# A mixture-of-experts layer: half the depth of the down product as three rounded products, the low part of its weights by GpSimd

## The chip, the cores and the metric

The kernel runs on one core of one Trainium2 chip. The metric is the device time of one execution in microseconds. Before the change it is 1408.04 us, the median of 3 runs (1407.59 to 1409.12). The profile is one further execution. PE is TensorE, DVE is VectorE, ACT is ScalarE, POOL is GpSimd and SP is the engine that issues most DMAs.

## The reference, cut to what matters

One encoder layer: a token mixer, and then a mixture of experts with top-8 routing over 64 experts and one shared expert. Only the routed experts are touched:

```
def expert_block(args):
    xb, e = args
    return (jax.nn.silu(xb @ we_gate[e]) * (xb @ we_up[e])) @ we_down[e]
```

There are 512 tokens of 1024 channels, so 4096 assignments; the hidden width of an expert is 256. `we_gate[e]` and `we_up[e]` are 1024x256, `we_down[e]` is 256x1024, all float32. Each result is scaled by its gate and summed per token.

## The kernel before

The function `experts` works through blocks of up to 128 tokens that go to one expert. There are 64 blocks, one for each expert, and here four more for experts with over 128 tokens: 68. For a block the kernel finds its token numbers with a one-hot product, gathers the tokens' rows from HBM (POOL, `gather`), turns them (PE, `turn_x`), multiplies them with gate and up (PE, `gate_up`), applies silu and the product (ACT `sigmoid`, DVE `silu` and `hidden`), turns the hidden rows (PE, `turn_hidden`, one turned tile per half k of the 256 hidden channels), multiplies with the down weights (PE, `down`), copies the result out of PSUM in two halves (ACT and DVE, `y_half`) and scatters the rows to HBM (POOL, `scatter`).

Gate and up products are made in parts: ACT rounds a float32 operand to the type fp32r (`high`), DVE subtracts that from the operand and rounds the rest (`low`), and PE adds high·high, low·high and high·low. Each of these is a rounded product. The down product is exact: both operands are float32.

Each engine has its own program, a list of stages with a lead: in step b the stage with lead 2 works on block b + 2. `steps` writes these lists out for the first blocks, runs the rest up to block 59 in a counted loop, and blocks 60 to 67 in a loop with conditions. There POOL also waits at the end of each step until the scatter of that step has landed (the argument `last` of `steps`, called by `scattered`). The order of a list is the order in which its engine works; nothing reorders it. Semaphores join the lists.

Weights stand in rings of four slots that SP fills: gate and up of block b once the products of block b - 4 are done, down likewise. Every gather and scatter has a one-element addition on POOL ahead of it, `carrier` (L2123), which carries the waits.

Of the kernel before, what the change touches and what calls it, by code (L numbers as in the profile page):

```python
# [20 lines left out]
F32R = mybir.dt.float32r  # L21
# [7 lines left out]
P = 128  # L29
# [40 lines left out]
class Memory:  # L70
# [1865 lines left out]
def plan_experts(nc, m, w, keep, moe):  # L1936
# [38 lines left out]
def experts(nc, w, keep, moe):  # L1975
# [4 lines left out]
    with ExitStack() as stack:  # L1980
# [9 lines left out]
        sig = m.sb("sig5", [P, 2, DE])  # L1990
        hid = m.sb("hid", [P, 2, DE])
        hT = m.sb("hT5", [P, 2, 2, P])
# [18 lines left out]
        s_h, s_hA = m.sem("p5_hidden_turned"), m.sem("p5_hiddenT")  # L2011
# [14 lines left out]
        def steps(engine, stages, last=None):  # L2026
# [89 lines left out]
        def _(pool):  # L2116
# [25 lines left out]
            steps(pool, [(4, gather), (0, scatter)], lambda b, u: scattered(pool, b, u))  # L2142

        @block.scalar
        def _(act):
# [10 lines left out]
            def sigmoid(b, u, first):  # L2156
                act.wait_ge(s_gu, b + 1)
                taken(act, s_hid, b, 2)
                act.activation(sig[:, u % 2, :], pgu[u % 2][:, 0:DE], ACT.Sigmoid).then_inc(s_sig, 1)
# [8 lines left out]
            def hiddenT(b, u, first):  # L2168
                act.wait_ge(s_h, b + 1)
                taken(act, s_y, b, 2)  # L2170
                act.activation(hT[:, u % 2, :, :], ph[:, 0:2 * P].rearrange("p (k s) -> p k s", k=2), ACT.Copy).then_inc(s_hA, 1)  # L2171
# [6 lines left out]
            steps(act, [(2, high(0)), (2, high(1)), (0, hiddenT), (2, high(2)), (2, high(3)), (1, sigmoid), (2, x_high), (0, y_half)])  # L2178

        @block.tensor  # L2180
        def _(pe):
# [28 lines left out]
            def turn_hidden(b, u, first):  # L2210
                pe.wait_ge(s_hid, b + 1)
                taken(pe, s_hA, b, 1)
                rows = hid[:, u % 2, :].rearrange("p (d k) -> p k d", k=2)
# [11 lines left out]
            def down(b, u, first):  # L2225
                pe.wait_ge(s_hA, b + 1)
# [3 lines left out]
                weights = moe.down[:, u % RING, :, :]  # L2230
# [279 lines left out]
```

## Time and profile before

| | |
|---|---|
| median of the runs | 1408.04 us |
| the profiled execution | 1406.37 us, span 1404.6 us |
| PE busy | 1297.7 us, 92% |
| DVE busy | 1010.8 us, 72% |
| ACT busy | 617.2 us, 44% |
| POOL busy | 256.0 us, 18% |
| blocks of the experts | about 650 to 1340 us of the span |
| exact down products, L2233 | 544 records, 8 for each block: 2 for each of 4 products |

A record of PE overlaps the next, so the time that a product takes from PE is the distance between two starts, not the length of a record. "idle before" stands in square brackets, with what ended the idle time. A row of the timeline can hold several instructions (x2); its length then reaches from the first start to the last end.

### The profile page before, as it was taken

What the parts mean: (1) busy time and instruction counts of PE and PEld (TensorE: products, weight loads), DVE (VectorE), ACT (ScalarE), POOL (GpSimd) and SP (SyncE); (2) the same over time, 40 slices, a digit from 0 to 9 for tenths busy, and PEclk for the clock granted to TensorE, in tenths of its full rate; (3) what the DMA queues carried; (4) which work ended last, traced back from release to release, by engine and by line L of the source; (5) the groups of instructions that cost most, each with busy time, mean ns of one, the idle gap of its engine ahead of it and who ended that gap; (6) DMA issues with size and microseconds to landing.
All of it is one profiled execution on the core that took longest, in us unless ns stands there. A gap on an engine that the chain in (4) does not pass through costs nothing. (4 is left out here: it accounts for less than half of the span.)

```text
span 1404.6 us, 18781 instructions
## 1 busy us (share of the span) xinstructions
PE 1297.7 (92%) x5779; PEld 914.4 (65%) x5779; DVE 1010.8 (72%) x1651; ACT 617.2 (44%) x944; POOL 256.0 (18%) x329
## 2 busy tenths in 40 slices
PE   4999999858998999969999999999999999999947
PEld 4878888546884444536767677676776767776613
DVE  5879999789343523646878888788887888878617
ACT  3523222542242013134656566565665656656401
POOL 0000000250000000012233232332323323232200
PEclk9899999979998999989999999999999999999979
DMA  9773353100017321328999999999999999989268
GB/s 351 279 255 132 110 173 113 60 1 1 1 61 288 110 90 60 150 103 325 347 356 351 349 358 349 356 350 359 381 380 363 344 343 348 351 321 328 105 260 346
DMA packets 86890, 340.82 MB, mean 243 GB/s; under 512 B 17122, under 2 KB 22452, under 8 KB 59708
## 3 DMA queue, kind: packets, MB, share of 16 engines
q1 hardware_dynamic: 66960, 306.51, 58.3%
q0 software_dynamic: 19584, 33.60, 6.6%
q8 instruction: 27, 0.44, 0.1%
q10 hardware_dynamic: 300, 0.11, 0.0%
q14 instruction: 19, 0.16, 0.0%
HBM read 333.87 MB, written 44.04 MB: 269 GB/s over the span
## 5 line engine op out<-in xcount | busy, mean ns | idle before, releaser
L2261 DVE TENSOR_TENSOR gate_up_low<-gate_up,gate_up_high 128x1024 fp32r<-128x1024 f32 x204 | 244.6, 1220 | 42.5 <-ACT gate_up_high L2152 42.5
L2233 PE MATMUL py<-down_ring,hT 128*128 128x512 f32 x544 | 250.0, 602 | 1.0 <-ACT hT L2171 0.9
L2194 PE MATMUL p_gate_up<-gate_up_high,x_hi 128*128 128x512 f32 x544 | 242.4, 446 | 5.3 <-DVE x_lo L2270 5.3
L2194 PE MATMUL p_gate_up<-gate_up_low,x_hi 128*128 128x512 f32 x544 | 216.8, 398 | 0.0
L2194 PE MATMUL p_gate_up<-gate_up_high,x_lo 128*128 128x512 f32 x544 | 215.4, 396 | 0.0
L2152 ACT ACTIVATE gate_up_high<-gate_up 128x1024 fp32r<-128x1024 f32 x204 | 203.7, 1051 | 0.3 <-PEq L1415 0.3
L2233 PEld LDWEIGHTS py<-down_ring,hT 128*128 128x128 f32 x544 | 98.0, 190 | 99.0 <-issue 98.9
L2194 PEld LDWEIGHTS p_gate_up<-gate_up_high,x_hi 128*128 128x128 f32 x544 | 103.9, 191 | 44.6 <-issue 20.9
L2123 POOL TENSOR_TENSOR carrier<-offsets 1x1 f32<-1x1 f32 x136 | 30.7, 226 | 517.8 <-DVE tokens L2279 471.1
L2194 PEld LDWEIGHTS p_gate_up<-gate_up_high,x_lo 128*128 128x128 f32 x544 | 103.5, 190 | 30.1 <-issue 11.0
L2176 ACT ACTIVATE y<-py 128x512 f32<-128x512 f32 x68 | 40.7, 599 | 180.1 <-PE py L2233 180.1
L2194 PEld LDWEIGHTS p_gate_up<-gate_up_low,x_hi 128*128 128x128 f32 x544 | 102.8, 189 | 24.0
L463 PE MATMUL pz<-h_hi,w_hi 128*128 128x512 f32 x288 | 116.1, 403 | 0.0
L2139 POOL DMA_INDIRECT expert_rows<-y,row_ids x68 | 111.3, 1636 | 20.3 <-issue 20.3
L463 PE MATMUL pz<-h_hi,ring_lo 128*128 128x512 f32 x288 | 112.4, 390 | 0.0
L463 PE MATMUL pz<-h_lo,w_hi 128*128 128x512 f32 x288 | 112.3, 390 | 0.0
L2261 DVE TENSOR_TENSOR gate_up_low<-x_again,gate_up_high 128x1024 fp32r<-128x1024 f32 x68 | 82.5, 1232 | 18.4 <-ACT gate_up_high L2152 18.3
L2165 ACT ACTIVATE x_hi<-px 128x512 fp32r<-128x512 f32 x136 | 73.9, 595 | 39.0 <-PE px L2207 39.0
L2270 DVE TENSOR_TENSOR x_lo<-px,x_hi 128x512 fp32r<-128x512 f32 x136 | 87.1, 681 | 1.5 <-ACT x_hi L2165 1.5
L583 DVE SCALAR_TENSOR_TENSOR co<-upad,taps,co 128x512 f32<-128x512 f32 x120 | 82.3, 742 | 1.1 <-ACT gates L366 1.1
L2207 PEld LDWEIGHTS px<-ident,xg 128*128 128x128 f32 x544 | 71.8, 192 | 10.9 <-DMA xg<-h_rows,tokens 4.6
L2130 POOL DMA_INDIRECT xg<-h_rows,tokens x68 | 73.0, 1074 | 23.5 <-issue 22.6
(361 smaller groups left out, 1928.6 us busy)
## 6 DMA issues: line engine op xcount, KB each, us to landing
down_ring<-in_we_down SPq DMA_DIRECT2D x68, 1024.0 KB, 9.5
gate_up<-in_we_gate SPq DMA_DIRECT2D x51, 1024.0 KB
gate_up<-in_we_up SPq DMA_DIRECT2D x51, 1024.0 KB
x_again<-in_we_gate SPq DMA_DIRECT2D x17, 1024.0 KB
x_again<-in_we_up SPq DMA_DIRECT2D x17, 1024.0 KB
ring<-in_w_in SPq DMA_DIRECT2D x8, 2048.0 KB, 7.9
ring<-in_w_ada SPq DMA_DIRECT2D x16, 1024.0 KB, 5.9
rows<-expert_rows SPq DMA_DIRECT2D x6, 2048.0 KB, 18.5
```

What stands on the lines that cost most here:

```text
L463: last = pe.matmul(pz[n % 3][:, :], weights, h[:, k, :], start=(k == 0 and i == 0), stop=(k == KD - 1 and i == 2))
L583: done[r] = link.sign(nc.vector.scalar_tensor_tensor(out=mix.co[:, r, :], in0=u, scalar=tap, in1=mix.co[:, r, :], op0=ALU.mult, op1=ALU.add))
L2130: pool.indirect_dma_start(moe.xg[:, u % 4, :], None, keep.h2_dram, bass.IndirectOffsetOnAxis(tokens[:, u % 4, 0:1], 0), bounds_check=last_ ...
L2139: pool.indirect_dma_start(moe.rows, bass.IndirectOffsetOnAxis(row_ids[:, u % 4, 0:1], 0), y[:, u % 2, :], None, bounds_check=last_row, oob ...
L2152: act.activation(w_hi[:, u % 2, :, piece(i), :], moe.gate_up[u % RING][:, :, piece(i), :], ACT.Copy).then_inc(s_hi, 1)
L2165: act.activation(x_hi[:, u % 2, 4 * half:4 * half + 4, :], px[half][:, :].rearrange("p (k s) -> p k s", k=4), ACT.Copy).then_inc(s_xhi, 1)
L2176: act.activation(y[:, u % 2, 0:N], py[0][:, :], ACT.Copy).then_inc(s_yA, 1)
L2194: mm = pe.matmul(pgu[u % 2][:, :], x[:, u % 2, k, :], weights, start=(k == 0 and n == 0), stop=(k == KD - 1 and n == 2))
L2207: mm = pe.transpose(px[k // 4][:, (k % 4) * P:(k % 4 + 1) * P], rows[:, k, :], keep.ident[:, :])
L2233: mm = pe.matmul(py[half][:, :], hT[:, u % 2, k, :], weights[:, k, half * N:half * N + N], start=(k == 0), stop=(k == 1))
L2261: V.tensor_tensor(moe.low[u % RING][:, :, piece(i), :], moe.gate_up[u % RING][:, :, piece(i), :], exact(w_hi[:, u % 2, :, piece(i), :]), A ...
L2270: V.tensor_tensor(x_lo[:, u % 2, ks, :], px[half][:, :].rearrange("p (k s) -> p k s", k=4), exact(x_hi[:, u % 2, ks, :]), ALU.subtract).th ...
```

## The change

Of the 256 hidden channels, half k = 0 of the down product is no longer exact. ACT rounds the 128x1024 weights of that half (`down_high`), POOL subtracts the rounded ones from them and writes the rest in place (`down_low`, in the ring slot itself, through a second name for the same memory). ACT copies the two turned halves apart: rounded for k = 0, exact for k = 1. DVE makes the low part of the turned half (`hidden_low`). PE makes the exact product of half k = 1 and then high·high, low·high and high·low of half k = 0. Tiles `hid`, `sig` and the turned hidden rows have one buffer in place of two. The lists of ACT and DVE have a new order, and POOL's list begins with `down_low`.

```diff
+        down_hi = m.sb("down_high", [P, D], F32R)
...
-                                        if last is not None and lead == 0:
+                                        if last is not None and code is stages[-1][1]:
                                             last(4 * turn + u, u)
...
+            def down_low(b, u, first):
+                pool.wait_ge(s_dhi, b + 1)
+                pool.tensor_tensor(moe.down_low[:, u % RING, 0, :], moe.down[:, u % RING, 0, :], exact(down_hi[:, :]),
+                                ALU.subtract).then_inc(s_dlo, 1)
+
+            steps(pool, [(0, down_low), (4, gather), (0, scatter)], lambda b, u: scattered(pool, b, u))
...
+                act.activation(hT_hi[:, :], ph[:, 0:P], ACT.Copy).then_inc(s_hA, 1)
+                act.activation(hT_exact[:, :], ph[:, P:2 * P], ACT.Copy).then_inc(s_hA, 1)
+
+            def down_high(b, u, first):
+                slot_done(act, moe.s_down, b, u, 16)
+                taken(act, s_y, b, 1)
+                act.activation(down_hi[:, :], moe.down[:, u % RING, 0, :], ACT.Copy).then_inc(s_dhi, 1)
...
-            steps(act, [(2, high(0)), (2, high(1)), (0, hiddenT), (2, high(2)), (2, high(3)), (1, sigmoid), (2, x_high), (0, y_half)])
+            steps(act, [(2, high(0)), (0, down_high), (2, high(1)), (0, hiddenT), (2, high(2)), (1, sigmoid), (2, x_high), (2, high(3)),
+                        (0, y_half)])
...
                 for half in range(2):
-                    for k in range(2):
-                        mm = pe.matmul(py[half][:, :], hT[:, u % 2, k, :], weights[:, k, half * N:half * N + N],
-                                       start=(k == 0), stop=(k == 1))
+                    pe.matmul(py[half][:, :], hT_exact[:, :], moe.down[:, u % RING, 1, half * N:half * N + N], start=True, stop=False)
+                pe.wait_ge(s_dhi, b + 1)
+                for half in range(2):
+                    pe.matmul(py[half][:, :], hT_hi[:, :], down_hi[:, half * N:half * N + N], start=False, stop=False)
+                pe.wait_ge(s_hV, b + 1)
+                for half in range(2):
+                    pe.matmul(py[half][:, :], hT_lo[:, :], down_hi[:, half * N:half * N + N], start=False, stop=False)
+                pe.wait_ge(s_dlo, b + 1)
+                for half in range(2):
+                    mm = pe.matmul(py[half][:, :], hT_hi[:, :], moe.down_low[:, u % RING, 0, half * N:half * N + N],
+                                   start=False, stop=True)
                 mm.then_inc(s_y, 1)
...
+            def hidden_low(b, u, first):
+                dve.wait_ge(s_hA, 2 * b + 2)
+                taken(dve, s_y, b, 1)
+                V.tensor_tensor(hT_lo[:, :], ph[:, 0:P], exact(hT_hi[:, :]), ALU.subtract).then_inc(s_hV, 1)
...
-            steps(dve, [(2, low(0)), (2, low(1)), (4, places), (2, low(2)), (1, silu), (1, hidden), (2, low(3)), (2, x_low), (4, numbers),
-                        (1, row_numbers), (0, y_half)])
+            steps(dve, [(2, low(0)), (2, low(1)), (4, places), (0, hidden_low), (1, silu), (2, x_low), (1, hidden),
+                        (4, numbers), (1, row_numbers), (2, low(2)), (2, low(3)), (0, y_half)])
```

On DVE one step of the written-out part reads so before (`column` and `hot` are the stage `places`, `tokens` and `row_ids` are numbers for the gather and the scatter):

```order
L2261 TENSOR_TENSOR gate_up_low<-gate_up,gate_up_high 128x2x512 x2
L2292 COPY column<-table_parts 128x36
L2294 TENSOR_TENSOR hot<-iota,place 128x512
L2261 TENSOR_TENSOR gate_up_low<-gate_up,gate_up_high 128x2x512
L2247 SCALAR_TENSOR_TENSOR sig<-p_gate_up,number,sig 128x256
L2255 TENSOR_TENSOR hid<-sig,p_gate_up 128x256
L2261 TENSOR_TENSOR gate_up_low<-gate_up,gate_up_high 128x2x512
L2270 TENSOR_TENSOR x_lo<-px,x_hi 128x512 x2
L2277 TENSOR_REDUCE number<-pid 128x3
L2279 TENSOR_TENSOR tokens<-number,offsets 128x1
L2283 TENSOR_TENSOR row_ids<-number,offsets 128x1
L2300 COPY y<-py 128x512
```

And the same step now:

```order
L2290 TENSOR_TENSOR gate_up_low<-gate_up,gate_up_high 128x2x512 x2
L2321 COPY column<-table_parts 128x36
L2323 TENSOR_TENSOR hot<-iota,place 128x512
L2329 TENSOR_TENSOR hT_low<-ph,hT_high 128x128
L2276 SCALAR_TENSOR_TENSOR sig<-p_gate_up,number,sig 128x256
L2299 TENSOR_TENSOR x_lo<-px,x_hi 128x512 x2
L2284 TENSOR_TENSOR hid<-sig,p_gate_up 128x256
L2306 TENSOR_REDUCE number<-pid 128x3
L2308 TENSOR_TENSOR tokens<-number,offsets 128x1
L2312 TENSOR_TENSOR row_ids<-number,offsets 128x1
L2290 TENSOR_TENSOR gate_up_low<-gate_up,gate_up_high 128x2x512 x2
L2334 COPY y<-py 128x512
```

The third and fourth subtraction of the gate and up weights have moved from between `hot` and `x_lo` to the end of the step, straight ahead of the copy of y, and the new `hT_low` follows `hot`.

On POOL the loop with conditions (blocks 60 to 67) reads before, for one step, with the one instruction (ISA) in which it waits for the scatter to land:

```order
L2123 TENSOR_TENSOR carrier<-offsets 1x1
L2130 DMA xg<-h_rows,tokens 128x1024
L2048 UNCONDITIONAL_BRANCH
L2048 COMPARE_AND_BRANCH
L2135 REGISTER_ALU
L2123 TENSOR_TENSOR carrier<-offsets 1x1
L2139 DMA expert_rows<-y,row_ids 4096x1024
L2075 ISA
```

And now, from one scatter to the next gather:

```order
L2147 DMA expert_rows<-y,row_ids 4096x1024
L2083 ISA
L2056 UNCONDITIONAL_BRANCH
L2056 REGISTER_ALU
L2056 COMPARE_AND_BRANCH
L2151 REGISTER_ALU
L2152 TENSOR_TENSOR down_low<-down_ring,down_high 128x1024
L2056 UNCONDITIONAL_BRANCH
L2056 REGISTER_ALU
L2056 COMPARE_AND_BRANCH
L2135 REGISTER_ALU
```

So `down_low` of a block stands behind the scatter of the block before, and in this loop also behind the wait for its landing (L2083, before L2075).

## Rows read from the trace of the kernel before

**Rows 1.** Stretches, us: busy time of each engine, granted PE clock, DMA share, GB/s.

```profile
900.00:1000.00 100.00, 100.00 (x449) 71.59 (x448) 81.11 (x136) 61.32 (x88) 31.90 (x40) 1.00 0.95 361
```

**Rows 2.** Timeline of TensorE: start us, us, engine, line, operation, [idle before].

```profile
900.34 0.19 PEld L2194 LDWEIGHTS p_gate_up<-gate_up_high,x_hi 128*128 128x128 f32 x1 [0.31 <-issue]
...
908.87 0.19 PEld L2233 LDWEIGHTS py<-down_ring,hT 128*128 128x128 f32 x1 [0.24 <-issue]
...
910.66 0.19 PEld L2194 LDWEIGHTS p_gate_up<-gate_up_high,x_hi 128*128 128x128 f32 x1 [0.31 <-issue]
...
912.40 0.39 PE L2194 MATMUL p_gate_up<-gate_up_high,x_hi 128*128 128x512 f32 x1
...
912.63 0.40 PE L2194 MATMUL p_gate_up<-gate_up_high,x_lo 128*128 128x512 f32 x1
```

**Rows 3.** Timeline of VectorE and ScalarE in the step that begins at 900.34.

```profile
901.01 0.69 DVE L2300 COPY y<-py 128x512 f32<-128x512 f32 x1 [0.55 <-PE py L2233]
...
901.49 2.00 ACT L2152 ACTIVATE gate_up_high<-gate_up 128x1024 fp32r<-128x1024 f32 x2
...
902.58 2.36 DVE L2261 TENSOR_TENSOR gate_up_low<-gate_up,gate_up_high 128x1024 fp32r<-128x1024 f32 x2 [0.87 <-ACT gate_up_high L2152]
...
904.94 0.68 DVE L2294 TENSOR_TENSOR hot<-iota,place 128x512 bf16<-128x512 f32 x1
...
907.59 1.08 ACT L2165 ACTIVATE x_hi<-px 128x512 fp32r<-128x512 f32 x2 [0.50 <-PE px L2207]
...
909.17 1.28 DVE L2270 TENSOR_TENSOR x_lo<-px,x_hi 128x512 fp32r<-128x512 f32 x2
```

**Rows 4.** Timeline of GpSimd: a scatter early on, and one in a later step.

```profile
665.11 1.01 POOL L2139 DMA_INDIRECT expert_rows<-y,row_ids  x1 [0.43 <-issue]
...
912.64 0.18 POOL L2123 TENSOR_TENSOR carrier<-offsets 1x1 f32<-1x1 f32 x1
...
912.98 2.00 POOL L2139 DMA_INDIRECT expert_rows<-y,row_ids  x1 [0.16 <-issue]
```

**Rows 5.** The page's groups: the scatter issue's count, busy us and mean ns.

```profile
L2139 POOL DMA_INDIRECT expert_rows<-y,row_ids x68 | 111.3, 1636 | 20.3 <-issue 20.3
```

**Rows 6.** Lines L792 and L808, durations in ns: least, median, most.

```profile
L792 POOL TENSOR_TENSOR zr<-zr,X x4: 1257/1261/3466, 291.0 to 296.8; 128x512 f32<-128x512 f32 x4
...
L808 POOL TENSOR_TENSOR aB<-aB,hop x3: 1047/1048/1128, 312.9 to 336.3; 128x512 f32<-128x512 f32 x3
```

**Rows 7.** Timeline of VectorE and GpSimd where both work from SBUF.

```profile
290.79 2.49 DVE L1267 TENSOR_TENSOR gate_r_and_bonus<-gate_r_and_bonus,zr 128x512 f32<-128x512 f32 x4
...
293.20 1.25 DVE L1270 TENSOR_TENSOR hop<-XT,mid_e 128x12 f32<-128x12 f32 x1
...
312.15 0.39 DVE L1298 TENSOR_TENSOR X<-X,rank 128x220 f32<-128x220 f32 x1
...
312.91 1.05 POOL L808 TENSOR_TENSOR aB<-aB,hop 128x512 f32<-128x512 f32 x1 [3.38 <-PE all_banks L1017]
313.01 1.20 DVE L1298 TENSOR_TENSOR X<-X,rank 128x231 f32<-128x231 f32 x1
...
641.47 2.35 DVE L2261 TENSOR_TENSOR gate_up_low<-x_again,gate_up_high 128x1024 fp32r<-128x1024 f32 x2
641.57 1.16 POOL L2123 TENSOR_TENSOR carrier<-offsets 1x1 f32<-1x1 f32 x1 [8.52 <-DVE tokens L2279]
```

**Rows 8.** Timeline of the last blocks: GpSimd's waits, and the last two down products.

```profile
1287.10 0.86 POOL L2123 TENSOR_TENSOR carrier<-offsets 1x1 f32<-1x1 f32 x1 [9.09 <-DMA expert_rows<-y,row_ids]
...
1297.99 0.29 POOL L2123 TENSOR_TENSOR carrier<-offsets 1x1 f32<-1x1 f32 x1 [6.60 <-DMA expert_rows<-y,row_ids]
...
1315.97 0.18 POOL L2123 TENSOR_TENSOR carrier<-offsets 1x1 f32<-1x1 f32 x1 [3.49 <-DVE y L2300]
...
1330.42 3.60 PE L2233 MATMUL py<-down_ring,hT 128*128 128x512 f32 x8
...
1335.19 3.69 PE L2233 MATMUL py<-down_ring,hT 128*128 128x512 f32 x8 [0.95 <-ACT hT L2171]
```

More of the change, by code:

```diff
@@ L77, in sb, with over @@
         return self.stack.enter_context(self.nc.sbuf_tensor(name, shape, dtype))
+    def over(self, name, shape, dtype, at):
+        return self.nc.alloc_sbuf_tensor_at(name, shape, dtype, offset=at)
     def bank(self, name, shape=None):
@@ L1946, in plan_experts @@
     moe.gate_up, moe.low = [moe.gate_up[i] for i in order], [moe.low[i] for i in order]
+    down_at = nc.sbuf_base
     moe.down = m.sb("down_ring", [P, moe.RING, 2, D])
+    moe.down_low = m.over("down_low", [P, moe.RING, 2, D], F32R, down_at)
     moe.place = m.sb("place", [P, NT, NE])
@@ L1989, in experts @@
         w_hi = m.sb("gate_up_high", [P, 2, 2, KD, DE], F32R)
-        sig = m.sb("sig5", [P, 2, DE])
-        hid = m.sb("hid", [P, 2, DE])
-        hT = m.sb("hT5", [P, 2, 2, P])
+        down_hi = m.sb("down_high", [P, D], F32R)
+        sig = m.sb("sig5", [P, DE])
+        hid = m.sb("hid", [P, DE])
+        hT_hi, hT_lo = m.sb("hT_high", [P, P], F32R), m.sb("hT_low", [P, P], F32R)
+        hT_exact = m.sb("hT_exact", [P, P])
         y = m.sb("y5", [P, 2, D])
@@ L2157, in sigmoid @@
                 act.wait_ge(s_gu, b + 1)
-                taken(act, s_hid, b, 2)
-                act.activation(sig[:, u % 2, :], pgu[u % 2][:, 0:DE], ACT.Sigmoid).then_inc(s_sig, 1)
+                taken(act, s_hid, b, 1)
+                act.activation(sig[:, :], pgu[u % 2][:, 0:DE], ACT.Sigmoid).then_inc(s_sig, 1)
             def x_high(b, u, first):
@@ L2169, in hiddenT @@
                 act.wait_ge(s_h, b + 1)
-                taken(act, s_y, b, 2)
-                act.activation(hT[:, u % 2, :, :], ph[:, 0:2 * P].rearrange("p (k s) -> p k s", k=2), ACT.Copy).then_inc(s_hA, 1)
+                taken(act, s_y, b, 1)
[3 more added lines that the diff above has]
+                slot_done(act, moe.s_down, b, u, 16)
+                taken(act, s_y, b, 1)
+                act.activation(down_hi[:, :], moe.down[:, u % RING, 0, :], ACT.Copy).then_inc(s_dhi, 1)
             def y_half(b, u, first):
@@ L2211, in turn_hidden @@
                 pe.wait_ge(s_hid, b + 1)
-                taken(pe, s_hA, b, 1)
-                rows = hid[:, u % 2, :].rearrange("p (d k) -> p k d", k=2)
+                if not (isinstance(b, int) and b == 0):
+                    pe.wait_ge(s_hA, 2 * b)
+                taken(pe, s_hV, b, 1)
+                rows = hid[:, :].rearrange("p (d k) -> p k d", k=2)
                 for k in range(2):
@@ L2246, in silu @@
                 dve.wait_ge(s_sig, b + 1)
-                V.scalar_tensor_tensor(out=sig[:, u % 2, :], in0=pgu[u % 2][:, 0:DE], scalar=number[:, u % 4, 0:1], in1=sig[:, u % 2, :],
+                V.scalar_tensor_tensor(out=sig[:, :], in0=pgu[u % 2][:, 0:DE], scalar=number[:, u % 4, 0:1], in1=sig[:, :],
                                        op0=ALU.mult, op1=ALU.mult).then_inc(s_t, 1)
@@ L2253, in hidden @@
                 dve.wait_ge(s_t, b + 1)
-                taken(dve, s_h, b, 2)
-                V.tensor_tensor(hid[:, u % 2, :], sig[:, u % 2, :], pgu[u % 2][:, DE:2 * DE], ALU.mult).then_inc(s_hid, 1)
+                taken(dve, s_h, b, 1)
+                V.tensor_tensor(hid[:, :], sig[:, :], pgu[u % 2][:, DE:2 * DE], ALU.mult).then_inc(s_hid, 1)
             def low(i):
```

7 lines of the change are left out of this document (3 added, 4 removed).

## The prediction

> **What bounds the kernel now.** I read the page first: PE is busy for 92% of the span, DVE for 72%, and the two costliest groups are the subtraction of the weights and the exact down product. The view by stretches then says what holds there: in 100 us PE is busy for 100.00 us, DVE for 81.11, ACT for 61.32 and POOL for 31.90, the clock is granted in full, and the DMA engines are busy for 0.95 of the time at 361 GB/s [rows 1]. The timeline gives the step: the first weight load of a step comes at 900.34 and at 910.66, so a block costs 10.32 us [rows 2], and it is PE that sets it. What PE pays for a product is the distance of two starts. A rounded 128x512 product costs 0.23 us (912.40 to 912.63); in the exact down product a record starts every 0.24 + 0.19 = 0.43 us, and there are two records a product, so 0.86 us each [rows 2]. DVE works 81.11% of 10.32 = 8.4 us a step and waits for ACT (0.87 us ahead of the first subtraction) and for PE (0.55 us ahead of the copy of y) [rows 3]; it is second, with some 2 us to spare, and POOL and ACT come far behind. DMA has 5%.
>
> **The change part by part.** *PE.* A block had four exact down products, 4 x 0.86 = 3.44 us. Now it has two exact and six rounded ones: 1.72 + 6 x 0.23 = 3.10. That takes 0.34 us from the step: 10.32 becomes 9.98, as long as nothing else is late. The step changes once from exact to rounded products, as before. Over 64 blocks that run at PE's pace this is 22 us; the other four are those of the tail below.
>
> *ACT.* One more 128x1024 rounding (two take 2.00 us [rows 3], so 1.0) and the turned rows in two copies in place of one (below 0.4 more). It had 61.32% of 10.32 = 6.3; 6.3 + 1.4 = 7.7 us of 9.98: it lies beside PE. But high part 1 now comes 1.0 us later. Counted from the first weight load of the step, ACT is at the two high parts from 901.49 - 900.34 = 1.15; so high part 0 ends at 2.15, the down part at 3.15, high part 1 at 4.15.
>
> *DVE.* `hT_low` is 128x128; the 128x220 addition took 0.39 [rows 7], I take 0.3 (0.15 to 0.4). 8.4 + 0.3 = 8.7 of 9.98: it fits, with 1.3 to spare. The new order puts the last two subtractions (2.36 the pair [rows 3]) ahead of the copy of y. x_hi comes at 7.25 and takes 1.08 [rows 3], so x_lo runs from 7.9 to 9.1; hid and the small number work end at about 9.9 (an estimate: some 0.8), the two subtractions at 12.1, the copy of y at 12.8, which is 2.8 in the next step where it was 1.36. PE needs x_lo at 9.98 and the last two low parts 3 us later; y's PSUM banks it needs only when its down product starts, at about 7.0 (10.32 less 3.44, and a little for the change of kind). So nothing is late by itself. The gather's wait (tokens) and the single buffers of hid and sig are no later than before in any way that PE sees.
>
> *POOL.* The new subtraction is 128x1024 from two SBUF operands. No such one is in the trace; the nearest are 128x512 at 1.05 and 1.26 us [rows 6], with 0.18 for one element [rows 4]. 0.18 + 2 x (1.05 - 0.18) = 1.9, 0.18 + 2 x (1.26 - 0.18) = 2.3. I take 2.2, nearer to the form with no repeated operand. That writing fp32r costs POOL nothing extra is not shown; twice that, 4.4, is my upper end. Its place is behind the scatter of the block before. A scatter issue takes 1.01 or 2.00 us [rows 4].
>
> *Who holds whom.* POOL and DVE disturb each other when both read two operands from SBUF. An addition on DVE that takes 0.39 took 1.20 when it began 0.10 us behind a POOL multiplication, and ended 0.25 after it [rows 7]. The other way, a one-element carrier took 1.16 in place of 0.18: it waited for the first of two DVE subtractions and got in ahead of the second [rows 7]. But a POOL multiplication that arrived behind the first of four DVE multiplications took 3466 ns where 1261 is usual [rows 6], and only the fifth DVE instruction was held (hop, 1.25 for 12 columns) [rows 7]. DVE instructions with an operand in PSUM (hT_low, silu, x_lo, hid, copy of y) are not slowed in any row. A scatter issue that starts under a subtraction takes 2.00 [rows 4]; the mean of 1636 ns over 68 [rows 5] says that about 64% did.
>
> So the place of `down_low` decides. After the copy of y (2.8) low part 0 runs to 4.0. POOL's carrier is held till then and ends at about 4.15. The scatter follows 0.16 or 0.43 later, as the two gaps are [rows 4]: at 4.3 or 4.6. Low part 1 starts at 4.2, when ACT is done. If the scatter is behind, it waits for 5.4 and ends at 6.4; `hot` (0.68) has run by 6.1, and `down_low` goes from 6.4 to 8.6 beside instructions that have an operand in PSUM. PE wants it behind 1.72 + 4 x 0.23 us of the down product that starts at 7.0, at 9.6. Nothing is late. I take this as the likelier, since 4.3 and 4.6 are behind 4.2 and 64% of the scatters now are under a subtraction, but the margin is a tenth of a microsecond.
>
> The Trainium skill, page "SBUF — State Buffer", section "SBUF: two separate sides", says that VectorE instructions with two SBUF inputs and GpSimd instructions that read SBUF share one pair of ports, that the first to start keeps it for its whole instruction, and that the other is blocked fully. The 1.20 agrees with that; the 3466 ns asks for more than the rule says, as three borders between DVE instructions went by. By the rule alone the side that POOL's subtraction falls on is the rival A below.
>
> *The tail.* In blocks 60 to 67 POOL waits at the end of each step until its scatter has landed: 9.09, 6.60 us behind the issue, and at most 3.49 once the weights are all there [rows 8]. Before, only the next gather was behind that wait. Now `down_low` of the next block is, and PE cannot end its down product without it. From one copy of y to the next the loop is: copy 0.7, start of POOL 0.25 to 0.5, carrier 0.2, gap 0.16 to 0.43, issue 1.0 to 1.8, landing 6.6 to 9.1, `down_low` 2.2, two rounded products 0.46, end of the product and start of the copy 0.5 to 0.7. That is 12.1 to 16.1, mid 14, against 10.3: 1.8 to 5.8 more, mid 3.7. It holds for blocks 61, 62 and 63, mid 11 us. Block 64 is behind a scatter with little traffic: 0 to 2, I take 1. Blocks 65 and 66 fit in their step. The last two down products are 1335.19 - 1330.42 = 4.8 us apart [rows 8], with nothing to multiply between; the loop with a landing of 3 is some 8.8: 4 more. In all 16 us, from 9 to 23.
>
> *Sum.* -22 + 16 = -6. The held instructions in the tail (`down_low` comes there when it will, and DVE's last subtractions wait up to 2.2 us for it) and in the first blocks get 3 together (0 to 8). That leaves -3: 1406.4 - 3 = 1403.4 for the profiled execution. The median of the runs is 1.7 above that execution, so 1405. The ends: -22 + 9 = -13, 1395; -22 + 23 + 8 = +9, 1417.
>
> **The rivals.** *A, slower: hot is held.* One mechanism: the scatter's issue slips in ahead of low part 1 and ends at 5.3; `down_low` waits for the end of low part 1 at 5.4 and has the ports until 7.6; `hot` then ends at 8.3 and not at 6.1. PE multiplies with `hot` (the token numbers) ahead of the down product, which was to start at 7.0; so PE waits 1.3 us in each step. The step is 11.3, 1.0 more than before; DVE too has then 8.7 + 2.2 = 10.9 us of work and holding, so it cannot fall back. 60 x 1.0 + 16 + 3 = 79: about 1487; if half of the steps go so, 1445. It decides at whether the scatter comes before 4.2. For it speak the carrier that won the border and the 36% of scatters that now find DVE free; against it the gaps of 0.16 and 0.43.
>
> *B, the tail costs little:* the landing is quick because POOL gets there earlier against the weight loads. -22 + 5: 1391. Against it: 9.09 was the first of the waits, just behind three weight loads.
>
> *C, DMA becomes the bound:* 0.95 x 10.32 = 9.8 us of DMA in a step is below 9.98, with 0.98 of the time busy. If 361 GB/s is all there is, against the 361 x 10.32 / 9.98 = 373 wanted, the static part gains nothing: 1408 + 16 + 3 = 1427; if half, 1416.
>
> *D, POOL writes fp32r at half the speed:* 4.4 us from 6.4 is 10.8, and two products later the step ends, at 11.2 or 0.9 over 10.32: 1408 + 60 x 0.9 + 16 + 10 = 1488.
>
> **How the numbers follow.** The forecast has 0.47, A 0.28 (half of it in all steps, half in a part of them), B 0.07, C 0.08, D 0.06, and 0.04 is left for what I do not see. A measurement of this kernel can tell about 0.2%, 2.8 us, from no change: 1405.2 to 1410.9 is "the same". Of the forecast's 0.47, whose own range is 1395 to 1417, I give 0.25 to faster, 0.13 to the same and 0.09 to slower. B adds 0.07 to faster, C 0.02 to faster, 0.03 to the same and 0.03 to slower; A and D are slower; the rest is split. Faster 0.36, same 0.18, slower 0.46. The range goes from 1394 to 1484: it leaves out B's lower part and the worst of A.
>
> **What would show it.** In the profile after: the exact down products x272 records and six rounded ones at 0.23; the first weight loads of two steps 9.98 apart (A: about 11.3, with PE idle ahead of the token-number product for DVE's `hot`); `down_low` near 2.2 us; `hot` at 0.68 (A: near 2.9); in the tail PE idle ahead of its last down products for POOL, and copies of y 12 to 16 us apart. I am wrong if the steps of the loop are not at 9.98, or if blocks 61 to 63 stay below 12.

## The result and the profile after

| | before | after |
|---|---|---|
| median of the runs | 1408.13 us (4 runs, 1407.59 to 1409.12) | 1535.79 us (4 runs, 1533.36 to 1537.29) |
| profiled execution, span | 1406.4, 1404.6 | 1537.29, 1535.5 |
| ratio to before | | 1.0904, 95% interval 1.0887 to 1.0920 |

The kernel became 9.0% slower where 1405 us was forecast; the range, 1394 to 1484, did not hold it. The view by stretches of after stands against [rows 1] (columns: us, share of each engine and its instructions, granted TensorE clock, DMA share, GB/s):

```profile
900.00:1000.00 100.00, 90.09 (x391) 66.26 (x390) 88.05 (x121) 57.58 (x89) 58.47 (x41) 0.93 0.79 291
1000.00:1100.00 100.00, 88.36 (x401) 65.40 (x400) 90.96 (x127) 59.49 (x92) 57.54 (x40) 0.97 0.88 325
```

PE was at 100.00 and is at 90.09; the clock is no longer granted in full; DMA fell from 0.95 to 0.79. DVE is close behind PE. The page's groups and the view of the waits say which instruction swelled and who waits for it:

```profile
L2290 DVE TENSOR_TENSOR gate_up_low<-gate_up,gate_up_high 128x1024 fp32r<-128x1024 f32 x204 | 349.6, 1736 | 49.6 <-ACT gate_up_high L2165 48.8 <-issue 0.6
L2152 POOL TENSOR_TENSOR down_low<-down_ring,down_high 128x1024 fp32r<-128x1024 f32 x68 | 164.9, 2426 | 41.2 <-DMA expert_rows<-y,row_ids 38.8 <-ACT down_high L2190 0.6
L2262 PE MATMUL py<-down_low,hT_high 128*128 128x512 f32 x136 | 46.8, 428 | 16.3 <-POOL down_low L2152 16.3
L2244 PE MATMUL pid<-column,hot 128*128 128x9 bf16 x272 | 17.4, 171 | 78.2 <-DVE hot L2323 78.2
```

DVE's subtraction of the gate and up weights has a mean of 1736 ns over 204; undisturbed it takes 1.22 us. PE waits 78.2 us for `hot`, and 16.3 us for `down_low`. Why the subtraction swells is seen in the timeline of POOL and DVE over one step (start, duration; in brackets the idle time before and its releaser):

```profile
923.05 1.01 POOL L2147 DMA_INDIRECT expert_rows<-y,row_ids  x1 [0.16 <-issue]
924.10 2.40 POOL L2152 TENSOR_TENSOR down_low<-down_ring,down_high 128x1024 fp32r<-128x1024 f32 x1
```
```profile
921.62 1.23 DVE L2290 TENSOR_TENSOR gate_up_low<-gate_up,gate_up_high 128x1024 fp32r<-128x1024 f32 x1
923.51 4.08 DVE L2290 TENSOR_TENSOR gate_up_low<-gate_up,gate_up_high 128x1024 fp32r<-128x1024 f32 x1 [0.67 <-ACT gate_up_high L2165]
...
927.59 0.68 DVE L2323 TENSOR_TENSOR hot<-iota,place 128x512 bf16<-128x512 f32 x1
```

The two first subtractions of a step are called low part 0 and low part 1 from here on. Low part 1 starts at 923.51, 0.46 us into the scatter's issue, and 0.59 before `down_low` starts at 924.10. It ends at 927.59, 1.09 after `down_low` (926.50). An undisturbed one takes 1.23. 2.85 us are lost, and `hot` is late by them. In other steps the scatter comes a little under low part 0, and then `down_low` (912.04, 2.49 us) starts 0.81 ahead of low part 1, which takes 2.77 (912.85) and also ends 1.09 after it. So the same 1.09 us is left behind `down_low` whether low part 1 started before it or after it: the head start of 0.59 did not shorten what was left. Of the 68 low parts 1 of this run, 37 took 4.1 us and 20 took 2.7 to 2.8. PE, the same stretch:

```profile
904.06 0.26 PE L2244 MATMUL pid<-column,hot 128*128 128x9 bf16 x4 [1.71 <-DVE hot L2323]
...
909.08 0.42 PE L2214 MATMUL p_gate_up<-gate_up_high,x_hi 128*128 128x512 f32 x1
916.35 0.26 PE L2244 MATMUL pid<-column,hot 128*128 128x9 bf16 x4 [0.37 <-DVE hot L2323]
928.33 0.26 PE L2244 MATMUL pid<-column,hot 128*128 128x9 bf16 x4 [1.72 <-DVE hot L2323]
```
```profile
904.06:906.06 2.00, 2.00 (x9) 1.06 (x9) 2.00 (x6) 0.36 (x1) 0.00 (x0) 0.85 1.02 430
906.06:908.06 2.00, 2.00 (x5) 1.19 (x5) 1.97 (x6) 0.00 (x0) 1.43 (x2) 0.50 0.99 422
910.00:912.00 2.00, 2.00 (x10) 1.60 (x9) 1.13 (x2) 2.00 (x3) 1.19 (x2) 1.00 0.74 219
...
916.35:920.30 3.95, 3.95 (x17) 2.61 (x18) 3.92 (x10) 1.96 (x4) 1.37 (x2) 1.00 1.03 357
```

PE idles 1.71 us for `hot`; behind that the granted clock is 0.50 (the level of 1.2 GHz) around 907 and 1.00 again by 910. Not every such wait is followed by it: of this run's 38 waits of 1.6 to 1.9 us for `hot`, 20 were, and the kernel gate_oldorder below waits 1.46 to 1.72 us in each step while its clock is granted at 1.00 from 700 to 1370. From the token-number product to the first rounded gate and up product behind it are 909.08 - 904.06 = 5.02 us (3.30 in the gate kernel below). But the next wait for `hot` is then only 0.37, and behind that one the clock stays at 1.00. So most of what the clock takes from PE comes out of PE's wait: the steps here are 12.29 and 11.98. In the steps with full clock DVE sets the pace. Its work in an undisturbed step of the changed program is 8.5 us (measured below), 2.85 are held and 0.67 it waits for ACT's high part: 12.0. Behind a drop of the clock DVE's copy of y comes late too (it waited 0.66 for PE at 909.39), and that step is one of those in which low part 1 takes 2.77. The loop's mean over 58 steps is 12.08 (10.32 before).

The tail has the other cost. POOL behind block 60 and 61, and PE there (against [rows 8]), then DVE's copies of y:

```profile
1382.09 1.01 POOL L2147 DMA_INDIRECT expert_rows<-y,row_ids  x1 [0.49 <-issue]
1394.20 2.33 POOL L2152 TENSOR_TENSOR down_low<-down_ring,down_high 128x1024 fp32r<-128x1024 f32 x1 [11.10 <-DMA expert_rows<-y,row_ids]
1411.13 2.33 POOL L2152 TENSOR_TENSOR down_low<-down_ring,down_high 128x1024 fp32r<-128x1024 f32 x1 [9.50 <-DMA expert_rows<-y,row_ids]
```
```profile
1396.59 1.22 PE L2262 MATMUL py<-down_low,hT_high 128*128 128x512 f32 x2 [6.30 <-POOL down_low L2152]
1413.51 1.22 PE L2262 MATMUL py<-down_low,hT_high 128*128 128x512 f32 x2 [4.94 <-POOL down_low L2152]
```
```profile
1367.22 0.68 DVE L2334 COPY y<-py 128x512 f32<-128x512 f32 x1
...
1397.95 0.69 DVE L2334 COPY y<-py 128x512 f32<-128x512 f32 x1 [5.83 <-PE py L2262]
1414.86 0.69 DVE L2334 COPY y<-py 128x512 f32<-128x512 f32 x1 [4.06 <-PE py L2262]
1430.09 0.68 DVE L2334 COPY y<-py 128x512 f32<-128x512 f32 x1
1443.20 0.68 DVE L2334 COPY y<-py 128x512 f32<-128x512 f32 x1
```

`down_low` of a block stands behind the landing of the scatter of the block before. Blocks 61 to 64 end 17.46, 16.91, 15.23 and 13.11 us after the one before (10.50, 10.31, 10.31, 10.16 before the change).

The account of the 130 us: the same copy of y is late by 2.4 us at block 0, 105.0 at block 59 and 130.6 at block 67. So what comes up to the first block costs 2.4, the loop 102.6, the tail 25.6. Below, "late at block 59" is always this figure against the profiled execution of before.

### The profile page after: what moved, and what is told of

It is laid out like the page before. It is cut to its first block and busy times, and to the rows that moved or that the text cites. A ratio compares the mean times of both kernels' runs of the same rounds, so it can differ in the third digit from the quotient of the medians.

```text
span 1535.5 us, 19663 instructions
## 1 busy us (share of the span) xinstructions
PE 1337.9 (87%) x5915; PEld 965.9 (63%) x5915; DVE 1160.7 (76%) x1719; ACT 678.9 (44%) x1080; POOL 518.1 (34%) x397
## 5 line engine op out<-in xcount | busy, mean ns | idle before, releaser
L2290 DVE TENSOR_TENSOR gate_up_low<-gate_up,gate_up_high 128x1024 fp32r<-128x1024 f32 x204 | 349.6, 1736 | 49.6 <-ACT gate_up_high L2165 48.8
L2131 POOL TENSOR_TENSOR carrier<-offsets 1x1 f32<-1x1 f32 x136 | 119.9, 882 | 354.0 <-DVE tokens L2308 322.9
L2214 PE MATMUL p_gate_up<-gate_up_high,x_hi 128*128 128x512 f32 x544 | 223.9, 412 | 4.0 <-DVE x_lo L2299 3.8
L2165 ACT ACTIVATE gate_up_high<-gate_up 128x1024 fp32r<-128x1024 f32 x204 | 215.0, 1056 | 0.3 <-PEq L1418 0.3
L2152 POOL TENSOR_TENSOR down_low<-down_ring,down_high 128x1024 fp32r<-128x1024 f32 x68 | 164.9, 2426 | 41.2 <-DMA expert_rows<-y,row_ids 38.8
L2253 PE MATMUL py<-down_ring,hT_exact 128*128 128x512 f32 x272 | 154.6, 697 | 3.2 <-ACT hT_exact L2185 1.8
L2290 DVE TENSOR_TENSOR gate_up_low<-x_again,gate_up_high 128x1024 fp32r<-128x1024 f32 x68 | 118.6, 1766 | 14.6 <-ACT gate_up_high L2165 14.3
L2138 POOL DMA_INDIRECT xg<-h_rows,tokens x68 | 122.4, 1800 | 11.0 <-issue 10.4
L2244 PE MATMUL pid<-column,hot 128*128 128x9 bf16 x272 | 17.4, 171 | 78.2 <-DVE hot L2323 78.2
L2256 PE MATMUL py<-down_high,hT_high 128*128 128x512 f32 x136 | 84.4, 706 | 0.0
```

Of the source, the lines that this page charges most:

```text
L2131: nc.gpsimd.tensor_tensor(carrier[0:1, place:place + 1], moe.offsets[0:1, 0:1], moe.offsets[0:1, 0:1], ALU.add).then_inc(semaphore, 1)
L2138: pool.indirect_dma_start(moe.xg[:, u % 4, :], None, keep.h2_dram, bass.IndirectOffsetOnAxis(tokens[:, u % 4, 0:1], 0), bounds_check=last_ ...
L2152: pool.tensor_tensor(moe.down_low[:, u % RING, 0, :], moe.down[:, u % RING, 0, :], exact(down_hi[:, :]), ALU.subtract).then_inc(s_dlo, 1)
L2165: act.activation(w_hi[:, u % 2, :, piece(i), :], moe.gate_up[u % RING][:, :, piece(i), :], ACT.Copy).then_inc(s_hi, 1)
L2214: mm = pe.matmul(pgu[u % 2][:, :], x[:, u % 2, k, :], weights, start=(k == 0 and n == 0), stop=(k == KD - 1 and n == 2))
L2253: pe.matmul(py[half][:, :], hT_exact[:, :], moe.down[:, u % RING, 1, half * N:half * N + N], start=True, stop=False)
```

## The experiments

The theory by then: DVE's second low part is held while `down_low` is queued or running, and the landing wait costs the tail. The rival to each is given in the expectations. Each run's ratio is to runs of the kernel before on the same chip, with its 95% interval.

**gate.** POOL's subtraction waits until the low part of the turned values is there, so that it can't meet low part 1 or `hot`.

```diff
             def down_low(b, u, first):
                 pool.wait_ge(s_dhi, b + 1)
+                pool.wait_ge(s_hV, b + 1)
```

> The changed kernel with one more wait: down_low on GpSimd starts only once hT_low of the same block is done on VectorE, which stands right behind hot in VectorE's list. Theory (GpSimd's subtraction takes the SBUF ports from VectorE's second weight subtraction, hot comes late and TensorE waits for it): with the wait, down_low runs beside instructions that have an operand in PSUM; the subtractions are back at 1.2 us, TensorE no longer waits for hot, steps are 10.0 us in place of 12.1, the last eight blocks still cost some 25 us. Total about 1415 us. Rival 1 (VectorE has simply too much to do, or the new order of its list is at fault): steps stay near 12, total 1530 or more, since a wait was added. Rival 2 (GpSimd's chain is too long: scatter, then 2.4 us): TensorE waits for down_low in place of hot, steps of 11 to 12, total 1470 to 1530.

1412.68 us, 1.0028 [1.0015, 1.0042]. Steps of 10.01; 16.0 us early at block 59, 7.8 late at block 67.

```profile
900.00:1000.00 100.00, 100.00 (x481) 76.93 (x481) 85.15 (x150) 71.31 (x110) 71.98 (x50) 1.00 0.96 375
```
```profile
907.60 1.01 POOL L2147 DMA_INDIRECT expert_rows<-y,row_ids  x1 [0.16 <-issue]
909.92 2.36 POOL L2153 TENSOR_TENSOR down_low<-down_ring,down_high 128x1024 fp32r<-128x1024 f32 x1 [1.31 <-DVE hT_low L2330]
```
```profile
907.65 1.23 DVE L2291 TENSOR_TENSOR gate_up_low<-gate_up,gate_up_high 128x1024 fp32r<-128x1024 f32 x1 [0.26 <-ACT gate_up_high L2166]
...
911.44 1.29 DVE L2300 TENSOR_TENSOR x_lo<-px,x_hi 128x512 fp32r<-128x512 f32 x2 [0.62 <-ACT x_hi L2179]
```

PE is at 100.00 again and the clock in full, with the same instructions, and POOL's subtraction takes 2.36 us (2.40 above). DVE's own work is 85.15% of 10.01 = 8.5 us. While `down_low` runs from 909.92 to 912.28, DVE does `sig` and `x_lo`, which read PSUM, at their usual 0.48 and 1.29. So one wait on a semaphore is worth 105.0 + 16.0 = 121 us at block 59: the whole of the loop's loss is where `down_low` falls. DMA gives 375 GB/s.

**memset.** Does POOL's reading do it, or its time? (`small()` is a one-element addition; the low part of the down weights is left out.)

```diff
-                pool.tensor_tensor(moe.down_low[:, u % RING, 0, :], moe.down[:, u % RING, 0, :], exact(down_hi[:, :]),
-                                ALU.subtract).then_inc(s_dlo, 1)
...
+                small()
+                pool.memset(exact(moe.down_low[:, u % RING, 0, :]), 0.0).then_inc(s_m, 1)
...
+                small()
+                pool.memset(exact(moe.down_low[:, u % RING, 0, :]), 0.0).then_inc(s_dlo, 1)
```

> The changed kernel with down_low's subtraction replaced on GpSimd by two memsets of the same 128x1024 slot, each behind a one-element addition (about 2.5 us together, as long as the subtraction's 2.4, but they read nothing). It leaves out the low part of the down weights, which are set to zero. Theory (reading two operands is what stops VectorE): the second weight subtraction takes 1.2 us again and the steps are 10.0; total about 1415. Rival 1 (VectorE's order or amount of work) and rival 2 (time on GpSimd): steps stay near 12, total about 1535.

1412.47 us, 1.0025 [1.0014, 1.0036]; steps of 10.01, 16.8 early at block 59.

```profile
908.17 0.95 POOL L2160 MEMSET down_low<- 128x1024 f32 x1
```
```profile
906.96 1.22 DVE L2301 TENSOR_TENSOR gate_up_low<-gate_up,gate_up_high 128x1024 fp32r<-128x1024 f32 x1 [0.26 <-ACT gate_up_high L2176]
908.10 1.05 DVE L2332 COPY column<-table_parts 128x36 bf16 x1
908.18 0.97 DVE L2334 TENSOR_TENSOR hot<-iota,place 128x512 bf16<-128x512 f32 x1
```

The step is as short as it gets, but a memset does not leave DVE alone: the first one ran from 908.17 to 909.12, and DVE's copy of the column, 0.17 us by itself, ended at 909.15. `hot`, which takes 0.68 by itself and reads both operands from SBUF, ended at 909.15 as well: counted from low part 1's start it came only 0.3 later than in gate, so the memset did not hold it for its whole time. It costs nothing here, within what PE allows. No memset met low part 1, which had ended when the first one began, so whether one would hold a subtraction of the weights is not shown; `hot` speaks against it. The tail came out as in gate, +4.6 us at block 67: POOL's time is enough for that.

**tail.** The wait for a landing only behind the last block, for both of the last scatters.

```diff
-                                            last(4 * turn + u, u)
+                                            with engine.If(count < 4 * turn + (u + 2)):
+                                                last(4 * turn + u, u)
```

> The changed kernel, with GpSimd's wait for the landing of a scatter only behind the last block, not behind each of the blocks 60 to 67. Theory: from the copy of y of block 59 to that of block 67 the changed kernel takes 102 us against 77 before, because down_low stands behind that wait; without it 12 us steps remain there for blocks 60 to 63, so some 12 to 15 us go: total about 1522. The steps of the loop stay at 12.1. Rival (the last blocks are long for the same reason as the others, held ports): nothing goes, 1535.

1519.71 us, 1.0793 [1.0771, 1.0814]. 105.4 late at block 59 as in the kernel after (105.0), 114.3 at block 67: the last eight blocks cost 8.9 in place of 25.6.

**both.** gate and tail together.

> The kernel after with both repairs: GpSimd's subtraction waits for the low part of the turned values, and the wait for a scatter's landing stands behind the last block only. If the two costs are separate (the held VectorE instruction in the loop, the landing waits in the last blocks), they add up: 1412.7 of the first repair less the 16 us that the second gave by itself, 1394 to 1400, with steps of 10.0 us in the loop and last steps of 12 to 13 us in place of 16 to 17. If the landing waits were only hiding other waits of the last blocks (VectorE again held there by GpSimd), the second repair gives little here: 1405 to 1412.

1388.22 us, 0.9862 [0.9846, 0.9879]. Better than either theory said: 18.1 early at block 59, 18.9 early at block 67. The landing waits were worth 24.5 us here by the medians (gate 1412.68), and 23.0 by the last eight blocks of the two profiles, not 16. In the kernel after they probably lay partly beside DVE's late steps: its last eight blocks still cost 8.9 without them (tail), against -0.8 here.

**dve_low.** The subtraction goes to DVE, between `hot` and `hT_low`; POOL has the list of before.

```diff
-            steps(dve, [(2, low(0)), (2, low(1)), (4, places), (0, hidden_low), (1, silu), ...
+            steps(dve, [(2, low(0)), (2, low(1)), (4, places), (0, down_low), (0, hidden_low), (1, silu), ...
```

> The changed kernel with down_low's subtraction made by VectorE, behind hot and ahead of hT_low; GpSimd's list is as before the change. Theory (GpSimd's 2.4 us cost VectorE 2.9, its own 1.2 would cost it 1.2): VectorE has 8.4 + 0.3 + 1.2 = 9.9 us of work and some 0.7 of waits, steps are 10.3 to 10.8, and the last blocks cost little: total 1410 to 1440. Rival 1 (the new order or the amount of work on VectorE is at fault): steps of 12 and more, above 1520.

1388.90 us, 0.9864 [0.9844, 0.9884]. It takes DVE 1.22 us and POOL 2.36. DVE is at 95.52% with PE at 100.00: nobody waits for it.

```profile
900.00:1000.00 100.00, 100.00 (x481) 76.97 (x480) 95.52 (x160) 71.22 (x111) 47.44 (x40) 1.00 0.96 375
```
```profile
908.19 1.22 DVE L2323 TENSOR_TENSOR down_low<-down_ring,down_high 128x1024 fp32r<-128x1024 f32 x1
```

**nolow.** PE's last product reads `down_high` in place of `down_low`; POOL's subtraction and PE's wait for it are left out.

```diff
-                    mm = pe.matmul(py[half][:, :], hT_hi[:, :], moe.down_low[:, u % RING, 0, half * N:half * N + N],
+                    mm = pe.matmul(py[half][:, :], hT_hi[:, :], down_hi[:, half * N:half * N + N],
```

> No low part of the down weights is made at all; TensorE's last product reads the high part in its place (the low part of the down weights is left out). It is the upper bound of what the change can give. If TensorE alone sets the step, as in the two repaired kernels, steps of 10.0 us and 1386 to 1390, the same as with the subtraction on VectorE. If VectorE's subtraction there cost something, this one is below it by 1 us or more in the last or first blocks: 1380 to 1386.

1389.59 us, 0.9869 [0.9853, 0.9886]: no different from both and dve_low. So 19 us is all that PE's part of the change gives here, and those two get it.

**before_tail**, the kernel before with tail's edit, and **dve_tail**, dve_low with it.

> The kernel before with the wait for a scatter's landing behind the last block only. No instruction of GpSimd but gathers and scatters stands behind these waits there, so by the theory that they cost only through down_low it stays within 2 us of 1408. If they held the last scatters and with them the last copies of y, it gains 3 to 8 us.

1408.29 us, 0.9997 [0.9987, 1.0006].

> The subtraction on VectorE, and the wait for a scatter's landing behind the last block only. If the landing waits cost only where TensorE waits for an instruction of GpSimd queued behind them, they cost nothing here: 1387 to 1390, as with the subtraction on VectorE alone. If they cost in the last blocks anyway (in the kernel before and in this one), 1378 to 1384.

1388.75 us, 0.9854 [0.9838, 0.9870]. In neither does the landing wait cost a measurable time: it cost only where `down_low` was queued behind it.

**gate_oldorder.** gate, with DVE's list as before and `hT_low` behind the places.

```diff
-            steps(dve, [(2, low(0)), (2, low(1)), (4, places), (0, hidden_low), (1, silu), (2, x_low), (1, hidden),
-                        (4, numbers), (1, row_numbers), (2, low(2)), (2, low(3)), (0, y_half)])
+            steps(dve, [(2, low(0)), (2, low(1)), (4, places), (0, hidden_low), (2, low(2)), (1, silu), (1, hidden), (2, low(3)), (2, x_low),
+                        (4, numbers), (1, row_numbers), (0, y_half)])
```

> The first repair (GpSimd's subtraction waits for the low part of the turned values) with VectorE's list in the order of before, the turned values' low part put behind the places. If the new order of VectorE's list is needed so that no wait lies on the path, steps of 10.3 to 10.8, 1430 to 1460. If VectorE's free 15% takes either order, steps of 10.0 and 1410 to 1415.

1526.29 us, 1.0827 [1.0809, 1.0845]: far above both answers. `hT_low` now releases POOL just ahead of low part 2:

```profile
910.41 2.39 POOL L2153 TENSOR_TENSOR down_low<-down_ring,down_high 128x1024 fp32r<-128x1024 f32 x1 [0.17 <-DVE hT_low L2330]
```
```profile
910.91 2.98 DVE L2291 TENSOR_TENSOR gate_up_low<-gate_up,gate_up_high 128x1024 fp32r<-128x1024 f32 x1 [0.66 <-ACT gate_up_high L2166]
```
```profile
906.18 0.47 PE L2215 MATMUL p_gate_up<-gate_up_high,x_hi 128*128 128x512 f32 x1 [1.65 <-DVE x_lo L2300]
```

Another subtraction is held (it too ends 1.09 behind `down_low`), PE waits for `x_lo` (1.5 us a step) in place of `hot`, and the loss is of like size. The step is 11.8 in the mean. The new order of DVE's list, with only instructions that read PSUM in the 2.4 us behind `hT_low`, is what gives the gate a place to put `down_low`. What the old order costs without the gate no run shows.

**spacer and copy.** What takes the ports from a subtraction that has begun? ("The ports" are, as in the prediction, what DVE and POOL share when both work from SBUF.) Between the scatter and `down_low` a one-element addition is put in both; copy has besides the last three lines of this diff, so that `down_low` is a copy of one operand, and leaves out the low part of the down weights.

```diff
             def down_low(b, u, first):
                 pool.wait_ge(s_dhi, b + 1)
+                carry_wait(s_c, b, 2)
...
-                pool.tensor_tensor(moe.down_low[:, u % RING, 0, :], moe.down[:, u % RING, 0, :], exact(down_hi[:, :]),
-                                ALU.subtract).then_inc(s_dlo, 1)
+                pool.tensor_copy(moe.down_low[:, u % RING, 0, :], exact(down_hi[:, :])).then_inc(s_dlo, 1)
```

> As the kernel after, with an addition of one element on GpSimd between the scatter's issue and the subtraction. Theory 1: a one-element instruction waits for the border between two instructions of VectorE, so the subtraction starts only when the second low part is done; that low part takes 1.2 us, and the comparison for the next block (hot) is what is held, for some 2.4 us: TensorE's token-number product then waits about 1.3 us a step, steps of 11.3, 1480 to 1495. Theory 2: the low part stops as soon as GpSimd's queue holds the subtraction, whatever stands between: low part 2.8 to 4.1 us again, steps of 12.0, 1530 to 1540.

1543.25 us, 1.0965 [1.0947, 1.0984]. Theory 1, which is the prediction's rule for small instructions, is wrong:

```profile
912.17 1.01 POOL L2148 DMA_INDIRECT expert_rows<-y,row_ids  x1 [0.16 <-issue]
913.22 0.18 POOL L2132 TENSOR_TENSOR carrier<-offsets 1x1 f32<-1x1 f32 x1
913.36 2.39 POOL L2154 TENSOR_TENSOR down_low<-down_ring,down_high 128x1024 fp32r<-128x1024 f32 x1
```
```profile
912.63 4.20 DVE L2292 TENSOR_TENSOR gate_up_low<-gate_up,gate_up_high 128x1024 fp32r<-128x1024 f32 x1 [0.67 <-ACT gate_up_high L2167]
```

The small addition took 0.18 although DVE's low part had started 0.59 before it; it waited for no border. The low part again ended 1.08 behind `down_low`.

> The subtraction becomes a copy of the high part by GpSimd, one operand in place of two, behind the same one-element addition (the low part of the down weights is replaced by the high part, so it is left out). If any reading instruction of GpSimd holds VectorE for as long as it runs, the comparison (hot) is held for the copy's 1 to 2 us: steps of 10.0 to 10.8, 1405 to 1460. If only two operands hold it, nothing is held and the loop has steps of 10.0 with column copies of 0.2 us: 1410 to 1414. In the kernel with memsets a column copy took 1.05 in place of 0.17 us while a memset ran, which speaks for the first.

1445.69 us, 1.0271 [1.0250, 1.0291]. The copy takes 1.03 us and holds DVE as the subtraction does. This kernel shows a low part that is not held and one that is, one step after the other (POOL, then DVE):

```profile
768.11 1.01 POOL L2148 DMA_INDIRECT expert_rows<-y,row_ids  x1 [0.16 <-issue]
769.46 1.03 POOL L2154 CAST down_low<-down_high 128x1024 fp32r<-128x1024 f32 x1
778.17 1.02 POOL L2148 DMA_INDIRECT expert_rows<-y,row_ids  x1 [0.16 <-issue]
779.34 1.03 POOL L2154 CAST down_low<-down_high 128x1024 fp32r<-128x1024 f32 x1
```
```profile
768.24 1.23 DVE L2291 TENSOR_TENSOR gate_up_low<-x_again,gate_up_high 128x1024 fp32r<-128x1024 f32 x1 [0.33 <-ACT gate_up_high L2166]
778.54 2.91 DVE L2291 TENSOR_TENSOR gate_up_low<-gate_up,gate_up_high 128x1024 fp32r<-128x1024 f32 x1 [0.58 <-ACT gate_up_high L2166]
```

Low part 1 that starts 0.13 us into the scatter's issue goes through in 1.23, and POOL waits for its end (rival A, with `hot` held by 1.0): steps of 10.1. At 778.54 it starts 0.37 into it and is held; from there on, up to block 53, it starts 0.46 into it in every step and the steps are 10.7 to 10.9. Of this kernel's starts the latest that is not held is 0.32 into the issue, the earliest that is held 0.34. All those that are held end 1.08 behind the copy, whenever they started.

**shift.** nolow, with 384 more columns on ACT ahead of `down_high`, so that low part 1 comes late in the scatter's issue and nothing is queued behind the scatter.

```diff
+                act.activation(down_hi[:, 0:3 * P], moe.down[:, u % RING, 0, 0:3 * P], ACT.Copy).then_inc(s_twice, 1)
+                act.wait_ge(s_twice, b + 1)
                 act.activation(down_hi[:, :], moe.down[:, u % RING, 0, :], ACT.Copy).then_inc(s_dhi, 1)
```

> The kernel in which no low part of the down weights is made (it leaves that part out), with one more copy of 384 columns by ScalarE ahead of down_high, so that VectorE's second low part starts 0.5 to 0.8 us after the scatter's issue on GpSimd began in place of 0.06. Theory 1: from about 0.35 us on, a scatter's issue by itself has the ports, and what follows on GpSimd only goes on with it: the low part then ends about 1.09 us after the end of the scatter, with a duration of 1.3 to 1.6 in place of 1.23. Theory 2: only the large instruction queued behind the scatter holds VectorE: 1.23 as before. Steps of 10.0 us and 1387 to 1392 by both.

1391.40 us, 0.9874 [0.9855, 0.9894].

```profile
915.05 1.01 POOL L2148 DMA_INDIRECT expert_rows<-y,row_ids  x1 [0.16 <-issue]
```
```profile
915.66 1.23 DVE L2287 TENSOR_TENSOR gate_up_low<-gate_up,gate_up_high 128x1024 fp32r<-128x1024 f32 x1 [0.81 <-ACT gate_up_high L2161]
```

0.61 us into the issue, and not held; over the loop these starts are 0.52 to 0.96 us into it, and all take 1.22 or 1.23. So it is not the scatter's issue by itself. The kernel after has one step that parts queued from ready: at block 59 `down_low` stands behind the scatter but waits for ACT's `down_high`, and the subtraction 0.64 us into the issue is not held.

```profile
1368.81 1.01 POOL L2147 DMA_INDIRECT expert_rows<-y,row_ids  x1 [0.39 <-issue]
1370.46 2.48 POOL L2152 TENSOR_TENSOR down_low<-down_ring,down_high 128x1024 fp32r<-128x1024 f32 x1 [0.64 <-ACT down_high L2190]
```
```profile
1369.45 1.23 DVE L2290 TENSOR_TENSOR gate_up_low<-x_again,gate_up_high 128x1024 fp32r<-128x1024 f32 x1 [1.55 <-ACT gate_up_high L2165]
```

The reading that fits all of these is that the instruction queued behind the scatter, if it is ready to go, has the ports from about a third of a microsecond into the issue, long before its own start in the trace, and that a low part which starts later than that waits from its start on. What POOL does in that time no run shows.

## Why the prediction was wrong

**The step that failed is the place of `down_low`.** The prediction's walk had the scatter "at 4.3 or 4.6", behind low part 1 at 4.2, waiting for the latter's end, and so `down_low` from 6.4 beside instructions with an operand in PSUM. Even where nothing is held (gate) the scatter's issue starts 0.05 ahead of low part 1 and takes 1.01 beside it; so `down_low` would be ready to go at low part 1's end, as in rival A. And that does not last. Blocks 0 and 55 of the kernel after go as rival A said (low part 1 takes 1.28 and 1.23, and the copy of the column ahead of `hot` 2.35 and 2.36), and in the very next step low part 1 is 0.46 into the issue and takes 4.1. With `hot` late PE's down product is late, and from ACT's copy of y to DVE's low part 0 are then 1.58 us in place of 2.00 (gate). ACT's high part 1 is done 3.44 behind that copy in both kernels, so it now comes 0.67 behind low part 0's end (0.26 in gate; the walk had 0.2): the scatter is 0.46 ahead, and low part 1 is caught. The margin of a tenth of a microsecond was named; the chance of 0.47 was too much for it.

**Rival A had the right wait at too small a price.** It said: `hot` late, PE idle 1.3 us ahead of the token-number product, step 11.3. PE's wait is 66.3 us over 53 steps, 1.25 a step. But A let low part 1 end first, and held only `hot`. In fact it is low part 1 that is held: 2.85 us lost in place of 2.2, and ACT's 0.67 of waiting comes on top. "DVE too has then 8.7 + 2.2 = 10.9" became 8.5 + 2.85 + 0.67 = 12.0, and DVE is the bound. 58 steps at 0.8 more than A's 11.3 are 45 us, and the tail has 10 more: 1542, against 1536. The clock at 1.2 GHz behind about half of the waits of 1.7 us was not foreseen at all; it adds 0.1 to 0.2 to the mean step (12.08 against the 11.97 of a step without it, or 12.14 if the two short steps of 10.5 and 10.8 at blocks 55 and 56 are left out).

**PE.** "10.32 becomes 9.98": 10.01 in gate, both, dve_low and nolow. Right. The -22 us was 3 to 4 too much: 0.31 x 58 = 18, and the last blocks gave next to nothing (both: 18.1 early at block 59, 18.9 at 67).

**DVE and ACT fit beside it.** 8.7 of 9.98 forecast, 8.5 measured; `hT_low` 0.28 for 0.3; ACT 71.31% of 10.01 = 7.1 for 7.7. Right, once nothing is held.

**POOL's subtraction.** 2.2 forecast, 2.43 in the mean, 2.36 undisturbed. Rival D (4.4) is out.

**The tail.** The mechanism was right (tail and both take the cost away), the term mis-sized: 16 forecast, at most 23, measured 25.6. Blocks 61 to 63 took 15.2 to 17.5 us, against "12.1 to 16.1": the landing waits were 11.10, 9.50 and 8.14, and the estimate had taken 6.6 to 9.1 from [rows 8]. Block 64 cost 3.0 for "1", the last 3.9 for "4". Rival B is out.

**DMA.** Rival C is out: with the step at 10.01 it gave 375 GB/s at a share of 0.96, where 361 had been the rate at 10.32.

**The rule.** The prediction weighed the Trainium skill, page "SBUF — State Buffer", section "SBUF: two separate sides": the first to start keeps the pair of ports for its whole instruction. That the loser stands still fully is what the runs show (1.09 us of low part 1 left behind `down_low`). By the starts in the trace the first does not keep it: low part 1 had started 0.59 before `down_low` and lost. The rule would hold if POOL's instruction behind a scatter, when ready, counted as started about 0.34 us into the scatter's issue; that the work left is 1.09 also where low part 1 starts behind `down_low` fits this, and no run shows it directly.

## What to carry to other kernels

Here a GpSimd subtraction or copy of 128x1024 from SBUF cost VectorE its own duration, or more, in the SBUF instruction that it met, and nothing beside instructions that read PSUM. So let its wait name an event behind which VectorE has only such instructions. One semaphore was worth 121 us here; with the same semaphore and VectorE's list in the order of before the kernel took 1526 us, against 1536 without it in the new order. If VectorE has the time, it does such a subtraction in half of GpSimd's time (1.22 for 2.36 us) and no such meeting can happen: that kernel was as fast as the repaired one (1388.90 and 1388.22). Before something is put on GpSimd, look for the waits at the end of its list: waits for landings that were free with nothing behind them cost 24.5 us with a matmul's operand behind them. And a walk that turns on 0.1 us between two queues should be priced for both sides evenly.

## What the hardware did that was not expected

- A VectorE subtraction that starts 0.34 us or later into a scatter's issue is held if a GpSimd instruction stands ready behind the scatter (the copy kernel; at 0.32 it is not), though that instruction starts only at 1.04 us in the trace. With nothing behind the scatter (0.61, 1.23 us), or with an instruction that still waits (0.64, 1.23 us), it is not held.
- A held subtraction ends 1.08 or 1.09 us behind GpSimd's instruction, whether it started before that one or after it.
- GpSimd's one-operand copy of 1.03 us holds a low part too (2.91 in place of 1.23). Its memset of 0.95 us held VectorE's copy of the column (1.05 in place of 0.17 us), but `hot` ended only 0.3 us late beside it.
- The meeting locks itself in: the copy kernel ran its first 12 steps at 10.0 to 10.3 us, was held once, and stayed at 10.7 to 10.9 for the next 41.
- Of 38 idle times of PE of 1.6 to 1.9 us, 20 were followed by a granted clock of 0.50; 19 of about 0.4 us were not, and neither were those of 1.46 to 1.72 us in each step of gate_oldorder.
